# A hybrid decoder block on one core: the input projection of the first two x tiles in two halves of the model width

## The chip, the cores and the metric

The kernel runs on one core of one Trainium2 chip. A core has five engines with queues of their own: TensorE (PE in the rows; its weight loads are PEld), VectorE (DVE), ScalarE (ACT), GpSimd (POOL) and SyncE (SP), which here issues the large DMAs. They meet through semaphores. The metric is the device time of one execution in microseconds; less is better.

## What is computed

One layer over x of 1024 rows by 1024 columns, all in f32. The reference, cut to what matters here:

```python
mod = (silu(c) @ w_ada + b_ada)                      # 1024 -> 6 * 1024
sh1, sc1, g1, sh2, sc2, g2 = split(mod, 6)
h = rms_norm(x, norm1_g) * (1 + sc1) + sh1
q, k, v, u = split(h @ w_in)                         # 512, 128, 128, 512 columns
q, k = rope(rms_norm(q)), rope(rms_norm(k))          # angles = positions * inv_freq
a = sliding_window_attention(q, k, v, sinks)         # window 128
p = (window_mean(u, 2/4/8/16) - u) @ pool_w * pool_scale
x = x + g1 * (concat(a, p) @ w_o)
h2 = rms_norm(x, norm2_g) * (1 + sc2) + sh2
x = x + g2 * (square(relu(h2 @ w_mlp_in)) @ w_mlp_out)
```

## The kernel before

TensorE's products keep f32 accuracy by three products each: every operand is split into a high part (a cast to fp32r) and a low part (the operand less its high part), and high*high, high*low and low*high are added in PSUM. The casts are mostly ScalarE's (hi_... functions), the low parts VectorE's (lo_...).

**Order.** Nothing schedules this program: each engine's instructions stand in the order in which its block writes them, and semaphores (wait_ge) join the engines. An engine that waits holds all that stands behind it.

**Tiles.** x is worked in eight tiles of 128 rows. For each: square and root mean (square_x on ScalarE, root_x on GpSimd), scale (scale_x), transposes on TensorE (turn_x), h from the transposed tile with a1 and b1, one scalar per row of the transposed tile (make_h on VectorE for columns 0 to 511, make_h_half on ScalarE for the others), high and low parts of h, and the projection to u, q and k/v over KD = 8 blocks of 128 of the model width. u runs through window sums (pool_windows, with band matrices that GpSimd makes at the start) and a pool product (pool_out); q and k through norm, rope and transposes (turn_qk) to scores.

**The front.** Before h exists, b1 = sh1 and a1 = (1 + sc1) * norm1_g are needed. Both are 1024 to 1024 products of silu(c) with slices of w_ada. VectorE adds them up from eight pieces each (add_piece, [128, 1024], acc for sh1 and acc_sc for sc1), and TensorE sums the 128 partitions with one-column products (column_sum, L2075). The list stream sets the order of the loads into 12 buffers: eight pieces of sh1, eight of sc1, then w_in's u columns (wu, 4 pieces of two blocks) and its q, k and v columns (wqkv, 8 pieces of one block); x tiles 0 and 1 are asked for after the eighth. So nothing is projected before both vectors are complete. TensorE then runs project_u_first (L2238), project_qkv_first (L2274) and the second tile's project_u and project; products nobody reads (keep_clock, L2070) fill some of its waits. The later adaLN vectors are summed by VectorE in add_job_pieces between its other work for the tiles, by three lists of piece numbers (first_pieces, between_pieces, late_pieces), and loaded by JOB_LOADS.

**Two late steps.** angles (L1210) makes the rope angles on VectorE when tile 0 has been projected; sines (L876) follows on ScalarE. The band matrices differ for tile 0 (the window is cut at the start of the sequence), so GpSimd first makes that form (band_of, L1855) and rewrites it after tile 0's windows.

## Time and profile before

| | us |
|---|---|
| median of 3 runs | 938.44 (938.17 to 939.15) |
| the profiled execution | 939.17 |
| its span | 937.4 |
| TensorE busy | 915.0 |
| VectorE busy | 650.2 |
| ScalarE busy | 495.1 |
| GpSimd busy | 361.7 |

The span is the time from the first to the last instruction of one profiled execution, whose own time is 939.17; all rows have their times from the span's start. Busy times of engines overlap. A row of the timeline gives start, duration, engine, line, operation, output and inputs, and in brackets how long the engine had been idle and what ended that. The granted clock is TensorE's: 1.00 is 2.4 GHz and 0.50 is 1.2 GHz. A duration of a merged row runs from the first start to the last end of its x instructions; an f32 product of 128 columns is two of them.

### The profile page before, as it was taken

What the parts mean: (1) busy time and instruction counts of PE and PEld (TensorE: products, weight loads), DVE (VectorE), ACT (ScalarE), POOL (GpSimd) and SP (SyncE); (2) the same over time, 40 slices, a digit from 0 to 9 for tenths busy, and PEclk for the clock granted to TensorE, in tenths of its full rate; (3) what the DMA queues carried; (4) which work ended last, traced back from release to release, by engine and by line L of the source; (5) the groups of instructions that cost most, each with busy time, mean ns of one, the idle gap of its engine ahead of it and who ended that gap; (6) DMA issues with size and microseconds to landing.
All of it is one profiled execution on the core that took longest, in us unless ns stands there. A gap on an engine that the chain in (4) does not pass through costs nothing.

```text
span 937.4 us, 12606 instructions
## 1 busy us (share of the span) xinstructions
PE 915.0 (98%) x4387; PEld 765.5 (82%) x4387; DVE 650.2 (69%) x1001; ACT 495.1 (53%) x869; POOL 361.7 (39%) x347
## 2 busy tenths in 40 slices
PE   2999999999999999999999999999999999999998
PEld 2888888887888888888888888888888888888886
DVE  6978987888645778556555654445786666799896
ACT  2657888887655546554455544536334444333331
POOL 8162322243323446988888888721000000000000
PEclk9899999999999999999999999999999999999999
DMA  9943232235122423746555553349999538996772
GB/s 357 371 170 95 91 114 90 91 106 188 45 90 90 134 69 123 243 162 197 188 176 169 176 184 131 115 172 332 349 339 320 196 102 289 317 302 209 258 248 94
DMA packets 92271, 175.54 MB, mean 187 GB/s; under 512 B 9320, under 2 KB 26288, under 8 KB 92208
## 3 DMA queue, kind: packets, MB, share of 16 engines
q1 hardware_dynamic: 92096, 174.70, 55.0%
q8 instruction: 35, 0.57, 0.2%
q14 instruction: 28, 0.23, 0.1%
q10 hardware_dynamic: 112, 0.04, 0.0%
HBM read 136.95 MB, written 37.75 MB: 186 GB/s over the span
## 4 chain that ended last, share of the span: by engine, by line
PE 92%; DVE 4%; DMA 2%; SPq 1%; issue 1%; ACT 1%; POOL 0%; DVEq 0%
PE psum L2060 27%; PE psum L2062 27%; PE psum L2061 27%; PE psum L2056 3%; DMA raw<-in_w_ada 2%; PE psum L2154 1%; PE psum L2155 1%; PE psum L2158 1%; PE psum L2140 1%; DVE w_o_lo L1372 1%; PE psum L2230 1%; PE psum L2200 1%; PE psum L2173 1%; PE psum L2236 1%; DVE probs L1337 1%
## 5 line engine op out<-in xcount | busy, mean ns | idle before, releaser
L1115 ACT CAST down_operands<-down_raw 128x1024 fp32r<-128x1024 f32 x96 | 100.9, 1054 | 151.9 <-PE psum L2062 54.6
L2060 PE MATMUL psum<-down_operands 128*128 128x512 f32 x448 | 174.3, 389 | 0.0
L2061 PE MATMUL psum<-down_operands 128*128 128x512 f32 x448 | 174.3, 389 | 0.0
L2062 PE MATMUL psum<-down_operands 128*128 128x512 f32 x448 | 174.3, 389 | 0.0
L1775 DVE TENSOR_TENSOR down_operands<-down_raw,down_operands 128x1024 fp32r<-128x1024 f32 x93 | 112.5, 1220 | 19.5 <-ACT down_operands L1115 18.9
L2060 PE MATMUL psum<-h2T,w_operands 128*128 128x512 f32 x272 | 106.0, 390 | 0.1
L2062 PE MATMUL psum<-h2T,w_operands 128*128 128x512 f32 x272 | 105.9, 389 | 0.0
L2061 PE MATMUL psum<-h2T,w_operands 128*128 128x512 f32 x272 | 105.8, 389 | 0.0
L2060 PEld LDWEIGHTS psum<-down_operands 128*128 128x128 f32 x448 | 84.1, 188 | 17.6
L2062 PEld LDWEIGHTS psum<-down_operands 128*128 128x128 f32 x448 | 84.1, 188 | 17.4
L2061 PEld LDWEIGHTS psum<-down_operands 128*128 128x128 f32 x448 | 84.1, 188 | 17.3
L2012 POOL TENSOR_TENSOR w_operands<-raw,w_operands 128x512 fp32r<-128x512 f32 x56 | 84.2, 1505 | 35.6 <-ACT w_operands L1063 35.6
L2062 PE MATMUL psum<-t_sums_hi,w_operands 128*128 128x512 f32 x168 | 65.4, 389 | 0.0
L2060 PE MATMUL psum<-t_sums_hi,w_operands 128*128 128x512 f32 x168 | 65.4, 389 | 0.0
L2061 PE MATMUL psum<-t_sums_lo,w_operands 128*128 128x512 f32 x168 | 65.4, 389 | 0.0
L2060 PEld LDWEIGHTS psum<-h2T,w_operands 128*128 128x128 f32 x272 | 51.1, 188 | 11.1 <-issue 0.5
L2061 PEld LDWEIGHTS psum<-h2T,w_operands 128*128 128x128 f32 x272 | 51.1, 188 | 10.6
L2012 POOL TENSOR_TENSOR w_operands<-w_sums,w_operands 128x512 fp32r<-128x512 f32 x42 | 55.3, 1329 | 11.3 <-ACT w_operands L1063 11.3
L2062 PEld LDWEIGHTS psum<-h2T,w_operands 128*128 128x128 f32 x272 | 51.1, 188 | 10.5
L1063 ACT CAST w_operands<-w_sums 128x512 fp32r<-128x512 f32 x42 | 26.1, 623 | 55.9 <-PE psum L2062 52.5
L2060 PE MATMUL psum<-w_o_hi,mixT_hi 128*128 128x512 f32 x128 | 51.2, 400 | 0.0
L2062 PE MATMUL psum<-w_o_hi,mixT_lo 128*128 128x512 f32 x128 | 50.0, 391 | 0.0
(285 smaller groups left out, 1960.9 us busy)
## 6 DMA issues: line engine op xcount, KB each, us to landing
down_raw<-in_w_mlp_out SPq DMA_DIRECT2D x160, 256.0 KB, 4.3
down_raw<-act_scratch SPq DMA_DIRECT2D x112, 256.0 KB, 3.3
raw<-in_w_ada SPq DMA_DIRECT2D x32, 512.0 KB, 4.6
raw<-in_w_mlp_in SPq DMA_DIRECT2D x32, 512.0 KB, 5.0
act_scratch<-act_quads_a SPq DMA_DIRECT2D x64, 256.0 KB, 2.3
act_scratch<-act_quads_b SPq DMA_DIRECT2D x48, 256.0 KB, 3.6
slots<-in_w_ada SPq DMA_DIRECT2D x8, 512.0 KB, 10.6
xh<-in_x SPq DMA_DIRECT2D x8, 512.0 KB, 5.7
```

Source lines behind the costliest of these rows:

```text
L1063: nc.scalar.copy(w1op[:, w1_slot(b, name), 0, :, :], w1_quad(b, quad)).then_inc(w1_hi, 1)
L1115: nc.scalar.copy(o[:, 0, :, :], r[:, 0:2, :]).then_inc(op2_hi, 1)
L1337: ins = v.tensor_tensor_reduce(out=pr[:, kv, h, 0:w], in0=banks(4)[:, 256 * h:256 * h + w], in1=mask[:, m0:m0 + w], scale=1.0, scalar=-3e3 ...
L1372: v.tensor_tensor(wol[:, k, :], piece_at(place[("wo", k)]), woh[:, k, :].bitcast(F32), ALU.subtract).then_inc(wo_lo_dve, 1)
L1775: v.tensor_tensor(o[:, 1, :, :], r[:, 0:2, :], f32(o[:, 0, :, :]), ALU.subtract).then_inc(op2_lo_dve, 1)
L2012: g.tensor_tensor(o[:, 1, :, :], quad, o[:, 0, :, :].bitcast(F32), ALU.subtract).then_inc(w1_lo, 1)
L2056: return nc.tensor.transpose(o, i, ident[0:rows_, 0:rows_])
L2060: mm(o, wh, ah, start=first, stop=False, skip_group_check=adds)
L2061: mm(o, wh, al, start=False, stop=False, skip_group_check=adds)
L2062: return mm(o, wl, ah, start=False, stop=last, skip_group_check=adds)
L2140: ins = mm(o, qT[:, kv * G + h, :], k_, start=a == 0, stop=a == 1)
L2154: mm(bank(0), h[:, k, :], wih[:, k, QKV:IN], start=k == 0, stop=False)
```

## The change

The front is cut in two halves of the model width. Each double piece now has 512 columns of sh1 and the same 512 of sc1 (stream's mod pieces). After eight of them a1 and b1 are complete for blocks 0 to 3, and TensorE projects x tiles 0 and 1 over those blocks (project_u_half, project_qkv_half), leaving the sums open in PSUM: tile 1 gets banks of its own (u_bank, q_bank, kv_bank). The other eight pieces are summed meanwhile, and a second pass over blocks 4 to 7 ends the sums (project_qkv_second, then the u halves). The loads are interleaved to match. ScalarE makes the first half of h for both tiles, VectorE the second half of tile 0 in two steps. angles goes on VectorE behind the first sums (with one product in place of eight), sines into the front on ScalarE. GpSimd takes three of the casts (wu 1, wqkv 1 and 3), and makes the general band and a 16-column form for tile 0's first columns, used by extra narrow products. Two casts stand around the second x tile's square. keep_clock stands at other places with other counts. The adaLN sums of sh2, sc2 and g1 get a buffer each, and their pieces, loads and reductions move to later tiles.

```diff
-        stream = [("sh1", k) for k in range(KD)]
-        stream += [("sc1", k) for k in range(KD)]
-        stream += [("wu", k) for k in range(KD // 2)]
-        stream += [("wqkv", k) for k in range(KD)]
+        stream = [("mod", k) for k in range(KD)]
+        stream += [("wu", 0), ("wu", 1)]
+        stream += [("wqkv", k) for k in range(NK)]
+        stream += [("mod", KD + k) for k in range(KD)]
+        stream += [("wqkv", k) for k in range(NK, KD)]
+        stream += [("wu", 2), ("wu", 3)]
...
-        JOB_LOADS = (4, 4, 4, 3, 4, 4, 1, 0)
+        JOB_LOADS = (4, 2, 3, 4, 4, 5, 2, 0)
+        job_sums = (slots[:, NT - 1, :], slots[:, NT - 2, :], acc[:, :])
+        POOL_CASTS = ((1,), (1, 3))
...
                 load(n)
-                if n == 7:
+                if n == 2:
                     load_x(0)
+                if n == place[("wu", 1)]:
                     load_x(1)
...
+            square_x(0)
+            scale_x(0)
+            hi_wu(0)
+            make_h_half(0, 0)
+            hi_h(0, 0)
+            hi_wqkv(0)
+            square_x(1)
+            hi_wqkv(2)
+            scale_x(1)
+            make_h_half(1, 0)
             hi_h(1, 0)
+            sines()
...
+            sum_front(0)
+            angles()
+            shift_1(0)
             scale_1(0)
-            make_h(0, 0)
+            lo_wu(0)
+            lo_wu(1)
+            lo_h(0, 0)
+            for k in range(NK):
+                lo_wqkv(k)
+            sum_front(1)
+            lo_wqkv(4)
+            shift_1(1)
             scale_1(1)
+            make_h_front()
...
-            first_pieces = ([], [], (5,), (8,), (12, 13), (16,), (18, 19), (22,))
-            between_pieces = ([], [], [], (9,), (14,), (17,), (20,), (23,))
-            late_pieces = ((0, 1, 2, 3), (4,), (6, 7), (10, 11), (15,), [], (21,), [])
+            first_pieces = ([], [], (2,), (5,), (9,), (13, 14), (18,), (22,))
+            between_pieces = ([], [], [], (6,), (10,), (15,), (19,), (23,))
+            late_pieces = ([], (0, 1), (3, 4), (7, 8), (11, 12), (16, 17), (20, 21), [])
...
-                if t in (3, 5):
+                if t in (4, 6):
...
+            for n, fill in ((3, 8), (4, 6)):
+                pe.wait_ge(mod_summed, n)
+                keep_clock(fill, 3)
+            turn_x(0)
+            for n, fill in ((5, 4), (6, 5), (7, 2)):
+                pe.wait_ge(mod_summed, n)
+                keep_clock(fill, 3)
             pe.wait_ge(mod_summed, KD)
...
+            ins.then_inc(sc1_turned, 1)
+            keep_clock(8, 3)
...
+            project_u_half(0, 0)
+            project_qkv_half(0, 0, (q_part(0), kv_part(0)))
+            project_u_half(1, 0)
+            project_qkv_half(1, 0, (q_part(1), kv_part(1)))
+            keep_clock(4, 2)
+            for n, fill in ((15, 4), (16, 2)):
                 pe.wait_ge(mod_summed, n)
                 keep_clock(fill, 2)
...
+            pe.wait_ge(b1_second, 1)
+            pe.wait_ge(a1_ready, 2)
+            turn_x(1, NK, KD)
+            project_qkv_second()
+            project_u_half(0, 1)
+            project_u_half(1, 1)
+            pe.wait_ge(u_kept, 1)
+            turn_x(2)
+            project_qkv_half(1, 1, (q_part(1),))
             pool_windows(0)
-            turn_x(2)
-            pe.wait_ge(q_gained, 1)
-            project(bank(6), 0, AW, 1).then_inc(q_done, 1)
+            project_qkv_half(1, 1, (kv_part(1),))
             pool_out(0)
```

How instructions stand, at three places. First TensorE ahead of its first projection product, before (xh is the x tile, ones the vector of the column sums, the products of ident alone are keep_clock's):

```order
L2076 MATMUL psum<-ones,acc 128x1 [waits mod_summed]
L2076 MATMUL psum<-ones,acc 128x1 x7
L2056 MATMUL psum<-ident,xh 128x128 [waits x_scaled]
L2056 MATMUL psum<-ident,xh 128x128 x7
L2056 MATMUL psum<-ident,xh 128x128 [waits x_scaled,cols_ready]
L2056 MATMUL psum<-ident,xh 128x128 x7
```

and now:

```order
L2147 MATMUL psum<-ident 128x128 x5
L2130 MATMUL psum<-ident,xh 128x128 [waits x_scaled]
L2130 MATMUL psum<-ident,xh 128x128 x7
L2147 MATMUL psum<-ident 128x128 [waits mod_summed]
L2147 MATMUL psum<-ident 128x128 x3
L2147 MATMUL psum<-ident 128x128 [waits mod_summed]
L2147 MATMUL psum<-ident 128x128 x4
L2147 MATMUL psum<-ident 128x128 [waits mod_summed]
L2147 MATMUL psum<-ident 128x128
L2150 MATMUL psum<-ones,acc 128x1 [waits mod_summed]
```

The transposes of x tile 0 and 25 fill products have moved ahead of the first column sums, and those of tile 1 are gone from here. Second, VectorE behind its first eight pieces, before:

```order
L1255 COPY cols<-psum 128x72 [waits rows_turned]
L1205 TENSOR_SCALAR squares<-slots,small 128x1024 [waits raw_in8,mod_summed]
L1207 SCALAR_TENSOR_TENSOR squares<-slots,small,squares 128x1024 [waits raw_in9,mod_summed]
L1207 SCALAR_TENSOR_TENSOR squares<-slots,small,squares 128x1024 [waits raw_in10,mod_summed]
L1207 SCALAR_TENSOR_TENSOR squares<-slots,small,squares 128x1024 [waits raw_in11,mod_summed]
```

and now, from the last step of the angles:

```order
L1282 TENSOR_SCALAR probs<-probs 128x64 [waits own_dve]
L1313 TENSOR_TENSOR small<-psum,cols 128x4 [waits mod_turned,cols_ready]
L1323 TENSOR_TENSOR small<-psum,cols 128x4 [waits sc1_turned]
L1326 SCALAR_TENSOR_TENSOR small<-small,cols 128x4 [waits own_dve]
L1357 TENSOR_TENSOR w_in_lo<-slots,w_in_hi 128x2x512 [waits wu_hi,raw_in8]
L1357 TENSOR_TENSOR w_in_lo<-slots,w_in_hi 128x2x512 [waits wu_hi_pool,raw_in9]
L1350 TENSOR_TENSOR hT_lo<-xh,hT_hi 128x512 [waits h_hi]
L1363 TENSOR_TENSOR w_in_lo<-slots,w_in_hi 128x768 [waits wqkv_hi,raw_in10]
L1363 TENSOR_TENSOR w_in_lo<-slots,w_in_hi 128x768 [waits wqkv_hi_pool,raw_in11]
L1363 TENSOR_TENSOR w_in_lo<-raw,w_in_hi 128x768 [waits wqkv_hi,raw_in0]
L1363 TENSOR_TENSOR w_in_lo<-raw,w_in_hi 128x768 [waits wqkv_hi_pool,raw_in1]
L1255 TENSOR_SCALAR squares<-raw,small 128x1024 [waits raw_in2]
```

The second eight pieces now stand behind a wait for TensorE's column sums and seven low parts. Third, GpSimd around the roots of x tiles 0 and 1, before (one root for both, after three bands):

```order
L1858 AFFINE_SELECT band<-band 128x16 [waits own_pool]
L1861 AFFINE_SELECT band<-band 128x16 [waits own_pool]
L1870 TENSOR_SCALAR small<-small 128x2 [waits x_squared,own_pool]
L1872 TENSOR_TENSOR small<-small 128x2 [waits own_pool]
L1883 MEMSET band 128x1 x15
```

and now, from the end of the second band's successor:

```order
L1932 TENSOR_TENSOR band<-band,ident 128x128 [waits own_pool]
L1952 CAST w_in_hi<-slots 128x2x512 [waits raw_in9]
L1936 TENSOR_SCALAR small<-small 128x1 [waits x_squared]
L1938 TENSOR_TENSOR small<-small 128x1 [waits own_pool]
L1956 CAST w_in_hi<-slots 128x768 [waits raw_in11]
L1956 CAST w_in_hi<-raw 128x768 [waits raw_in1]
```

The root of tile 0 stands after two bands of five operations each; the second root is a wait of its own with two casts behind it.

## Rows read from the trace of the kernel before

**Rows 1.** The page: the span, and TensorE's clock in 40 slices.

```profile
span 937.4 us, 12606 instructions
PEclk9899999999999999999999999999999999999999
```

**Rows 2.** TensorE's waits, 0 to 110: line, releaser, us in total, times, longest.

```profile
PE psum L2076 <- DVE acc L1207: 3.5, 1, 3.5
...
PE psum L2056 <- DVE kT L1367: 0.5, 1, 0.5
```

**Rows 3.** The timeline, TensorE up to its first projection product.

```profile
20.57 3.68 PE L2056 MATMUL psum<-ident,xh 128*128 128x128 f32 x16 [0.81 <-ACT xh L725]
...
24.04 2.08 PE L2073 MATMUL psum<-ident 128*128 128x128 f32 x14
...
28.39 1.83 PE L2076 MATMUL psum<-ones,squares 128*128 128x1 f32 x15
...
31.95 2.07 PE L2230 MATMUL psum<-w_in_hi,hT_hi 128*128 128x512 f32 x4 [0.61 <-ACT hT_hi L744]
```

**Rows 4.** Windows: length, busy times, granted clock, DMA share, GB/s.

```profile
31.00:32.00 1.00, 0.39 (x5) 0.20 (x3) 0.96 (x4) 0.90 (x3) 0.00 (x0) 0.64 1.07 398
32.00:33.00 1.00, 1.00 (x3) 0.81 (x4) 1.00 (x2) 1.00 (x4) 0.00 (x0) 0.50 1.03 399
...
38.00:39.00 1.00, 1.00 (x5) 0.77 (x4) 1.00 (x2) 1.00 (x3) 0.00 (x0) 0.95 1.03 402
```

**Rows 5.** The timeline, VectorE: sums, low parts of u, of h, of qkv, angles.

```profile
12.22 3.93 DVE L1207 SCALAR_TENSOR_TENSOR acc<-slots,small,acc 128x1024 f32<-128x1024 f32 x3
...
33.17 1.22 DVE L1294 TENSOR_TENSOR w_in_lo<-slots,w_in_hi 128x1024 fp32r<-128x1024 f32 x1
34.31 0.69 DVE L1287 TENSOR_TENSOR hT_lo<-xh,hT_hi 128x512 fp32r<-128x512 f32 x1
...
37.29 3.56 DVE L1300 TENSOR_TENSOR w_in_lo<-slots,w_in_hi 128x768 fp32r<-128x768 f32 x4
...
52.17 0.74 DVE L1225 SCALAR_TENSOR_TENSOR probs<-probs 128x64 f32<-128x64 f32 x3
```

**Rows 6.** The timeline, ScalarE: first square, a cast of h, a half tile.

```profile
15.37 1.06 ACT L720 ACTIVATE pooledT<-xh 128x1024 bf16<-128x1024 f32 x1 [12.76 <-DMA xh<-in_x]
...
31.28 0.62 ACT L744 CAST hT_hi<-xh 128x512 fp32r<-128x512 f32 x1
31.80 1.50 ACT L734 ACTIVATE xh<-psum,small 128x128 f32<-128x128 f32 x4
```

**Rows 7.** The timeline, GpSimd: one operation in a gap of VectorE, one beside its sums.

```profile
7.85 0.29 POOL L1861 TENSOR_SCALAR_AFFINE_SELECT band<-band 128x128 f32<-128x128 f32 x1
...
12.43 1.23 POOL L1858 TENSOR_SCALAR_AFFINE_SELECT band<-band 128x128 f32<-128x128 f32 x1
```

**Rows 8.** The timeline, TensorE: tile 1's first u products, tile 2's first.

```profile
48.85 0.40 PE L2154 MATMUL psum<-w_in_hi,hT_second 128*128 128x512 f32 x1
...
49.09 0.39 PE L2155 MATMUL psum<-w_in_lo,hT_second 128*128 128x512 f32 x1
...
65.98 0.47 PE L2154 MATMUL psum<-w_in_hi,hT_hi 128*128 128x512 f32 x1
```

**Rows 9.** DMA queues from 8 to 9: packets, MB, share; q10 is ScalarE's.

```profile
q10 hardware_dynamic: 6, 0.00, 0.6%
```

**Rows 10.** The instructions on acc: GpSimd's cast of 1024 columns.

```profile
L1913 POOL CAST g_hi<-acc x1: 1042/1042/1042, 193.0 to 193.0; 128x1024 fp32r<-128x1024 f32 x1
```

**Rows 11.** Windows: tile 4, after 120.

```profile
120.00:143.00 23.00, 23.00 (x148) 20.48 (x147) 20.20 (x55) 19.67 (x49) 6.42 (x9) 1.00 0.34 114
```

More of the change, by code:

```diff
@@ L323, in build @@
         out_quad = [sem("out_quad0"), sem("out_quad1"), sem("out_quad2")]
-        own = {e: sem(f"own_{e}") for e in ("act", "dve", "pool")}
+        own = {e: sem(f"own_{e}") for e in ("dve", "pool")}
         block = ctx.enter_context(nc.Block())
@@ new lines, in sum_front @@
+            def sum_front(half):
+                sums = acc_sc if half else acc
+                for k in range(KD):
+                    if k >= 1:
+                        dve.wait_ge(mod_summed, front_summed(KD * half + k - 1))
+                    if k < KD - 1:
+                        add_piece(sums[:, :], ("mod", KD * half + k), k, mod_summed)
+                    else:
+                        a = landed(dve, ("mod", KD * half + k))
+                        for m in range(2):
+                            cut = slice(512 * m, 512 * m + 512)
+                            v.scalar_tensor_tensor(out=sums[:, cut], in0=a[:, cut], scalar=silu[:, k:k + 1],
+                                                   in1=sums[:, cut], op0=ALU.mult, op1=ALU.add).then_inc(mod_summed, 1)
+                    if half == 0 and k == 1:
+                        dve.wait_ge(rows_in, 16 * 4)
+                        v.tensor_copy(rows[64:72, :], posi[64:72, :]).then_inc(posf_ready, 1)
+                    if half == 0 and k == 2:
+                        dve.wait_ge(rows_turned, 1)
+                        v.tensor_copy(cols[:, :], psum[:, 0, 0:72]).then_inc(cols_ready, 1)
+                    if half == 1 and k == 1:
+                        lo_h(1, 0)
@@ L1875, in _, with hi_wqkv @@
+            def hi_wqkv(k):
+                a = landed(pool, ("wqkv", k))
+                g.tensor_copy(wih[:, k, 0:QKV], a[:, 0:QKV]).then_inc(wqkv_hi[1], 1)
+            inv = np.float32(ROPE_THETA) ** (-np.arange(0, ROT_DIM, 2, dtype=np.float32) / np.float32(ROT_DIM))
+            for f in range(HALF):
+                ins = g.memset(inv_row[:, f:f + 1], float(inv[f]))
+            ins.then_inc(ident_made, 1)
             for i, w in enumerate(POOL_WINDOWS):
-                own_p.step(g.memset(band[:, i, 0:P], 1.0 / w))
+                own_p.step(g.memset(band[:, i, :], 1.0 / w))
@@ L1877, in _ @@
+            for s in range(MAX_WINDOW):
+                own_p.step(g.memset(band_first[:, s:s + 1], float(np.float32(1.0) / np.float32(s + 1))))
             own_p.wait()
-            for i, w in enumerate(POOL_WINDOWS):
-                if i == NP - 1:
-                    pool.wait_ge(x_squared, 2)
-                    root(rx[:, 0:2], ssx[:, 0:2], D, x_root)
-                for s in range(w - 1):
-                    own_p.step(g.memset(band[:, i, s:s + 1], float(np.float32(1.0) / np.float32(s + 1))))
-                own_p.wait()
-                band_of(i, band[:, i, 0:P], 0)
-                own_p.step(less_token(i, P))
-                own_p.wait()
-                own_p.step(g.memset(band[:, i, P:BAND], 1.0 / w))
-                own_p.wait()
-                band_of(i, band[:, i, P:BAND], P)
+            own_p.step(g.affine_select(out=band_first, in_=band_first, compare_op=ALU.is_ge, fill=0.0, base=0,
+                                       pattern=[[1, MAX_WINDOW]], channel_multiplier=-1))
@@ L2216, in _, with hi_hi, lo_hi @@
-            turn_x(1)
-            keep_clock(3, 2)
-            for n, fill in ((13, 4), (14, 4), (15, 2)):
+            pe.wait_ge(mod_summed, KD + 1)
+            for k in range(NK):
+                ins = column_sum(bank(2)[:, k:k + 1], acc, NK + k)
+            ins.then_inc(sc1_turned, 1)
+            keep_clock(8, 3)
+            def hi_hi(o, t, k, a, b):
+                return mm(o, hT(t)[0][:, k, :], wih[:, k, a:b], start=k == 0, stop=False)
+            def lo_hi(o, t, k, a, b):
+                return mm(o, hT(t)[1][:, k, :], wih[:, k, a:b], start=False, stop=False)
@@ new lines, in project_qkv_half @@
+            def project_qkv_half(t, half, parts):
+                pe.wait_ge(h_hi, h_step(t, half))
+                for k in range(NK * half, NK * half + NK):
+                    if (t, k) == (0, 3):
+                        turn_x(1, 0, NK)
+                    hi_made(pe, wqkv_hi, k)
+                    for o, a, b, _ in parts:
+                        hi_hi(o, t, k, a, b)
+                    pe.wait_ge(h_lo, h_step(t, half))
+                    for o, a, b, _ in parts:
+                        lo_hi(o, t, k, a, b)
+                    pe.wait_ge(wqkv_lo, k + 1)
+                    for o, a, b, done in parts:
+                        ins = hi_lo(o, t, k, a, b)
+                        if k == KD - 1:
+                            ins.then_inc(done, 1)
```

435 lines of the change are left out of this document (221 added, 214 removed).

## The prediction

> **What bounds the kernel now.** I read the page first: the span is 937.4 us and its PEclk row is 9 in nearly every slice [rows 1], so TensorE works almost without a break and anything that makes its dense work start earlier shifts the whole kernel. Then TensorE's waits before 110 us [rows 2]: behind the wait for the first transpose, which costs nothing by itself, stand the first column sums (3.5 us on VectorE's sums), and after that only waits under a microsecond. Then the timeline: until 31.95 TensorE does only column sums, transposes and products that nobody reads; the first projection product stands at 31.95 and from there no gap is seen [rows 3]. Last the windows of the clock [rows 4]: the mean is 0.64 at 31 to 32, 0.50 at 32 to 33 and 0.95 at 38 to 39, so the first projection runs some 6.2 us at half clock (1.2 GHz instead of 2.4), which costs 3.1 us. The yardstick for the change is the stretch from 31.95 to 65.98, where the third x tile's u projection starts [rows 8]: 34.0 us. What follows it is the same work in both kernels.
>
> **The start of the first half.** The transfers of 512 KB land 1.29 us apart (the first before the sum at 5.07, x tile 0 as the ninth just before its square at 15.37 [rows 6]). Now x tile 0 is the fourth and lands at 8.9; the eighth double piece lands at 15.3. VectorE's sums run at 1.31 us each (3.93 for 3 [rows 5]) and end at 17.3. The row vectors land on ScalarE's queue between 8 and 9 us [rows 9], so their cast, now after piece 1, ends at 8.9 and delays nothing by more than the copy.
>
> TensorE then has 14 clock-keeping products from the third sum on (10.4), the 8 transposes, 11 more products and 8 column sums before anything can be scaled. A pass takes 0.23 us at half clock and about 0.12 at full (3.68 for 16 transposes against 2.08 for 14 passes, two passes to a product [rows 3]). The clock rose about 3.9 us after the transposes began at 20.57 (PEclk reads 1.00 there, but the passes fall from 0.23 to 0.15), and 6.2 us after 31.95; from 10.4 that gives 14.3 to 16.6, and I take 15.7. The 14 products then end at 16.5, transposes 17.5, 11 products at 0.245 at 20.2, column sums (8 at 0.24) at 22.1. The root of x must be there by 16.5. GpSimd has ten band operations ahead of it. An operation that meets a sum takes 1.23 us instead of 0.29 [rows 7]; seven of ten so give a root at about 13.6 and the scaled tile at 14.7: not last. Bounds: all ten slow give 16.0 and 17.1, 0.6 us late. From 22.1: two small VectorE steps 0.5, ScalarE's half tile 1.50 and cast 0.62 [rows 6]: first product at **24.8**, 7.2 us earlier than before. The angles (about ten steps of 0.2 to 0.25 us, 0.74 for three [rows 5]) lie between 17.3 and 19.7, under TensorE's fill; if that cover were gone they would cost 2.4.
>
> **The first half itself.** Per tile 12 products each of u and q at 0.2275 (48.85 to 49.09 and on [rows 8]) and 12 of k and v at 0.12: 6.9 us, for two tiles 13.8. VectorE after 22.6: low parts of u twice 1.2, of h 0.7, of the qkv pieces 0.9 each [rows 5]. The second and fourth qkv casts stand on GpSimd behind the root of x tile 1, and that behind ScalarE's square, which now comes after cast 0: root at 27.5, cast of 768 columns 0.8 (1024 take 1.04 [rows 10]). VectorE waits 1.9 us for it; the bounds are 0 and 2.7. TensorE meets little of that (0.1), but x tile 1 is transposed only before the fourth piece (30.8), so ScalarE has its half cast at 33.5, and TensorE waits 1.2. First half ends at **40.4**, all at full clock.
>
> **Between the halves.** VectorE starts the second sums at 31.2: 0.8, low part of h 0.7 with 0.3 wait, six at 1.31 and a split one of 1.4: 42.2. Data is not last: the pieces land up to 34. TensorE has 10 more products (2.45) after 40.4 and stands at 42.9, 0.7 us behind the sums it could already have taken. Column sums 44.8, two small steps with their hand-overs 45.5, first two blocks of h 46.2, cast 0.4: second half starts at **46.7**. The gap is 6.2 us. Before, there was none. Here is where the early start goes.
>
> **The second half** is 13.8 us, x tile 2's transposes 0.9, windows 1.1 (now 1.4, four more narrow products), pool product 1.0 and the transposes of q and k 0.7, with 0.5 of waits for the high parts of h and of qkv piece 7: third u projection at **65.1**. ScalarE's queue (square of x 2 ahead of the squares of q) and the load of x 2, which now waits for the low part of the second half (47.8) and is 2.5 to 5 us under way, would stall it only if x 2 came after 55; I take nothing, bound 0 to 1.5.
>
> The sum against 31.95 to 65.98: start -7.2, half clock gone -3.1, gap +6.2, waits in the first half +1.3, transposes of x tile 1 now inside +1.0, windows +0.3, waits in the second half +0.5, rounding +0.1: **-0.9 us**. Off the path and free: the freed fix-up of the bands on GpSimd, the table load for the sines (covered by ScalarE's wait for h), the reordered loads. The profiled execution took 939.17 with its span of 937.4, against a median of 938.44; I take the difference off the median: 937.5 (a profiled execution would show 938.3, its span 936.5).
>
> **Later tiles.** Four adaLN sums leave VectorE's third-tile stretch and come back in tile 5 (five where two stood), and the reductions move from tiles 3 and 5 to 4 and 6. VectorE is busy 20.20 of 23 us at 120 to 143, TensorE 23.00 [rows 11]. One reduction (1.3) leaves 1.5 there. The waits that could vanish are 0.5 (kT) [rows 2]. I take 0, bounds -0.5 and +1.5.
>
> **A rule against it.** In the trace the clock rose while TensorE did only transposes (20.57 on [rows 3]). The Trainium skill, TensorE: Matmul & The Clock Gate, Part 4, says that transpose mode does not count as busy the same way; this trace disagrees. By the rule the stretch between the halves would hold only one-column sums and four idle transposes, which is the second rival.
>
> **The rivals.**
> 1. *The clock falls at the first half (slower).* Before, it fell at 31.3, after eight column sums (28.39 [rows 3]), four fill products and 0.6 us of waiting; now the same with eight fill products and 1.1 us of waiting. If it falls, 6.2 us at half clock cost 3.1, first half ends at 43.4 and everything follows: +2.1, **940.6**. It decides by whether eight fill products are enough. For it: the same pattern. Against: 11 products ahead of the sums and twice the fill.
> 2. *It falls between the halves.* 42.9 to 46.7 holds sums, waits and four transposes. Cost, since part hides under the waits for high parts, 2.2: **939.7**. Against: dense products stand on both sides.
> 3. *More overlap (faster).* The clock rises at 14.3 and the GpSimd cast is not waited for: first product 24.0, VectorE's sums end at 39.5, and TensorE's own work is last; with the first x tile's wait of 1.2 gone too, the second half starts at 44.8: -2.8, **935.6**.
> 4. *VectorE in tiles 4 to 6* becomes late: +1.5 on the sum, **939.0**.
> That the split changes nothing because weights land late is excluded by the landings above.
>
> **How the numbers follow.** Likeliest 0.42: 937.5, with 936.2 to 939.2 as its own range. Rival 1 0.20, rival 2 0.10, rival 3 0.22, rival 4 0.06. A measurement of this kernel can tell about 0.2% (1.9 us) from no change, so the line is at 936.6 and 940.3. Faster: 0.12 of the first case and 0.21 of rival 3, 0.33. Slower: 0.18 of rival 1, 0.05 of rival 2, 0.02 each of the first and rival 4, 0.27. Same 0.40. The range leaves out about a tenth on each side: 934.8 to 941.2.
>
> **What would show it.** First projection product near 24.8 (below 24: rival 3; above 26: GpSimd's root was late). Granted clock 1.00 from there to the end (rival 1: 0.50 for six windows). A gap of projection products between about 40.4 and 46.7, ended by column sums; if VectorE's sums end before 41, the fill products are the cost. Third u projection at 65.1. Most wrong I would be if the gap is under 3 us, or if both halves run at half clock.

## The result, and the profile of the changed kernel

| us | before | changed |
|---|---|---|
| median of 14 runs each | 937.51 (936.66 to 939.15) | 939.53 (937.73 to 940.45, and one of 3304.46) |
| the same two kernels, measured again | 937.33 (30 runs) | 939.31 (10 runs) |
| ratio | | 1.002, 95% interval 1.0012 to 1.0027; measured again 1.001 to 1.003 |
| third u projection at full clock (variants with wide column sums) | 63.72 | 64.98 |

The changed kernel is 2.0 us slower; 0.9 us faster was forecast. One run of the first comparison took 3304.46 us and was the profiled one; so the profile after is that of the same kernel measured again: 940.12 us, span 938.4, mean granted clock 0.998. The last line of the table is explained with the experiments.

The span and the clock in 40 slices, from the page of the changed kernel. They answer to [rows 1]; the 8 in the second slice is gone, yet the span is longer.

```profile
span 938.4 us, 12712 instructions
PEclk9999999999999999999999999999999999999999
```

TensorE up to the third u projection, from the timeline of the changed kernel (start, duration, engine, line, operation, output and inputs, count, and in brackets the idle time before and what ended it). These rows answer to [rows 3, 8].

```profile
11.27 6.21 PE L2147 MATMUL psum<-ident 128*128 128x128 f32 x28 [0.87 <-DVE acc L1257]
17.31 1.04 PE L2130 MATMUL psum<-ident,xh 128*128 128x128 f32 x8
18.18 2.62 PE L2147 MATMUL psum<-ident 128*128 128x128 f32 x22
20.64 1.84 PE L2150 MATMUL psum<-ones,acc 128*128 128x1 f32 x16
22.34 2.03 PE L2147 MATMUL psum<-ident 128*128 128x128 f32 x16
25.12 1.19 PE L2311 MATMUL psum<-w_in_hi,hT_hi 128*128 128x512 f32 x4 [0.75 <-ACT hT_hi L785]
...
34.61 1.20 PE L2311 MATMUL psum<-w_in_hi,hT_second 128*128 128x512 f32 x4 [1.29 <-ACT hT_second L785]
...
41.72 2.39 PE L2147 MATMUL psum<-ident 128*128 128x128 f32 x20
43.95 1.84 PE L2150 MATMUL psum<-ones,squares 128*128 128x1 f32 x16
46.36 0.63 PE L2130 MATMUL psum<-ident,xh 128*128 128x128 f32 x4 [0.57 <-DVE small L1316]
47.57 2.66 PE L2311 MATMUL psum<-w_in_hi,hT_hi 128*128 128x512 f32 x8 [0.59 <-ACT hT_hi L792]
...
67.23 0.47 PE L2231 MATMUL psum<-w_in_hi,hT_hi 128*128 128x512 f32 x1
```

The first projection product stands at 25.12 (31.95 before), so the front does start early. The first half runs to 41.72. Then come ten products nobody reads (x20 passes), the second column sums at 43.95, four transposes and, at 47.57, the second half. A stretch of 5.85 us holds no projection product and the kernel before had no such stretch. The third u projection stands at 67.23 against 65.98 [rows 8].

The clock at the start of the second half, from the windows of the changed kernel (window, length, busy time of PE, PEld, DVE, ACT, POOL with counts, granted clock, DMA share, GB/s), answering to [rows 4]:

```profile
46.00:47.00 1.00, 0.63 (x4) 0.42 (x4) 0.87 (x5) 0.00 (x0) 0.00 (x0) 1.00 0.00 0
47.00:48.00 1.00, 0.43 (x2) 0.38 (x3) 1.00 (x4) 0.65 (x2) 0.00 (x0) 0.95 0.00 0
48.00:49.00 1.00, 1.00 (x5) 0.90 (x4) 1.00 (x2) 1.00 (x3) 0.00 (x0) 0.50 0.00 0
...
51.00:52.00 1.00, 1.00 (x6) 0.81 (x6) 1.00 (x2) 1.00 (x4) 0.00 (x0) 0.84 0.88 336
```

The half clock (1.2 GHz) has not gone; in this execution it stands in the second half, 47.9 to 51.3, and not in the first projection. Before the fall TensorE did column sums, waited, did four transposes and waited again.

VectorE around its second eight pieces, from the timeline of the changed kernel:

```profile
28.65 1.48 DVE L1363 TENSOR_TENSOR w_in_lo<-slots,w_in_hi 128x768 fp32r<-128x768 f32 x1 [1.78 <-POOL w_in_hi L1956]
...
41.80 1.42 DVE L1296 SCALAR_TENSOR_TENSOR squares<-slots,small,squares 128x512 f32<-128x512 f32 x2
...
45.83 0.16 DVE L1316 TENSOR_TENSOR small<-psum,cols 128x4 f32<-128x4 f32 x1 [1.75 <-PE psum L2150]
```

The sums end at about 43.1, and TensorE takes them at 43.95, behind its fill.

### The profile page after: what moved, and what is told of

Read it like the earlier page. It is cut to its first block, busy times and chain, and to the rows that moved or that the text cites. A ratio compares the mean times of both kernels' runs of the same rounds, so it can differ in the third digit from the quotient of the medians.

```text
span 3302.7 us, 12712 instructions
## 1 busy us (share of the span) xinstructions
PE 3288.9 (100%) x4447; PEld 1833.7 (56%) x4447; DVE 657.0 (20%) x988; ACT 500.5 (15%) x875; POOL 341.2 (10%) x331
## 4 chain that ended last, share of the span: by engine, by line
PE 100%; DMA 0%; DVE 0%; ACTq 0%; issue 0%; ACT 0%
PE psum L2135 28%; PE psum L2134 27%; PE psum L2136 27%; PE psum L2130 4%; PE psum L2215 2%; PE psum L2231 1%; PE psum L2235 1%; PE psum L2232 1%; PE psum L2147 1%; PE psum L2314 1%; PE psum L2311 1%; PE psum L2317 1%; PE psum L2284 1%; PE psum L2251 1%; PE psum L2188 0%; PE psum L2190 0%
## 5 line engine op out<-in xcount | busy, mean ns | idle before, releaser
L2134 PE MATMUL psum<-down_operands 128*128 128x512 f32 x448 | 492.7, 1100 | 0.0
L2135 PE MATMUL psum<-down_operands 128*128 128x512 f32 x448 | 492.4, 1099 | 0.0
L2136 PE MATMUL psum<-down_operands 128*128 128x512 f32 x448 | 486.3, 1085 | 0.0
L2135 PE MATMUL psum<-h2T,w_operands 128*128 128x512 f32 x272 | 298.9, 1099 | 0.0
L2136 PE MATMUL psum<-h2T,w_operands 128*128 128x512 f32 x272 | 298.2, 1096 | 0.0
L2134 PE MATMUL psum<-h2T,w_operands 128*128 128x512 f32 x272 | 296.2, 1089 | 0.0
L2135 PEld LDWEIGHTS psum<-down_operands 128*128 128x128 f32 x448 | 196.8, 439 | 173.7 <-issue 173.7
L2134 PEld LDWEIGHTS psum<-down_operands 128*128 128x128 f32 x448 | 190.0, 424 | 180.7 <-issue 180.7
L2136 PEld LDWEIGHTS psum<-down_operands 128*128 128x128 f32 x448 | 189.0, 422 | 173.1 <-issue 173.1
L2135 PE MATMUL psum<-t_sums_lo,w_operands 128*128 128x512 f32 x168 | 184.5, 1098 | 0.0
L2136 PE MATMUL psum<-t_sums_hi,w_operands 128*128 128x512 f32 x168 | 184.4, 1098 | 0.0
L2134 PE MATMUL psum<-t_sums_hi,w_operands 128*128 128x512 f32 x168 | 182.9, 1088 | 0.0
L2136 PEld LDWEIGHTS psum<-h2T,w_operands 128*128 128x128 f32 x272 | 118.1, 434 | 105.4 <-issue 105.4
L2135 PEld LDWEIGHTS psum<-h2T,w_operands 128*128 128x128 f32 x272 | 116.2, 427 | 108.5 <-issue 108.5
L2134 PEld LDWEIGHTS psum<-h2T,w_operands 128*128 128x128 f32 x272 | 114.8, 422 | 106.0 <-issue 105.9
L2134 PE MATMUL psum<-w_o_hi,mixT_hi 128*128 128x512 f32 x128 | 143.5, 1121 | 0.0
L2136 PE MATMUL psum<-w_o_hi,mixT_lo 128*128 128x512 f32 x128 | 140.2, 1095 | 0.0
L2135 PE MATMUL psum<-w_o_lo,mixT_hi 128*128 128x512 f32 x128 | 140.2, 1095 | 0.0
L2136 PEld LDWEIGHTS psum<-t_sums_hi,w_operands 128*128 128x128 f32 x168 | 73.4, 437 | 65.4 <-issue 65.4
```

Source lines behind the costliest of these rows:

```text
L2134: mm(o, wh, ah, start=first, stop=False, skip_group_check=adds)
L2135: mm(o, wh, al, start=False, stop=False, skip_group_check=adds)
L2136: return mm(o, wl, ah, start=False, stop=last, skip_group_check=adds)
```

## The experiments

Three causes could be behind the missing 2.9 us. The fill products, in the front and in the gap, may hold TensorE up. The clock may have been mis-sized on both sides: worth less in the kernel before than the 3.1 us credited, and lost again between the halves. Or the later tiles may have become slower (theory B in the expectations).

Ten runs of one kernel lie up to 3.5 us apart, mostly by the clock, so a difference between two medians is uncertain by about 1 us; the smaller ones below are carried by the rows and not by the medians.

The later tiles could be dropped from the two traces alone: from the third u projection to the end of the span the changed kernel takes 938.4 - 67.23 = 871.2 us, the kernel before 937.4 - 65.98 = 871.4.

**The changed kernel again** (no edit).

> The changed kernel once more, to read its rows. Theory A (the clock): TensorE runs a few us of the first half at half clock, so the granted clock of the whole execution is 0.998 or 0.996 and the span 937 to 939; the first projection product stands near 24.8 and the third u projection between 65.1 (never at half clock) and 67.2. Theory B (later tiles): the front ends near 65.1 at full clock and the loss of 1 to 2 us is in TensorE waits between 70 and 230.

Measured: 939.31 against 937.33. All rows above are from this run.

**The kernel before again** (no edit, one execution), since its first profile was one execution out of many.

> The kernel before once more, to read its clock in another execution. If its usual half-clock stretch at the first projection is 6.8 us, as in the profiled execution of 939.2 us, the granted clock is 0.996 and the time near 939; if it is usually 3.4 us, 0.998 and near 937.4. The second would mean that 1.7 us of the clock gain I counted was mostly not there to be had.

Its timeline, TensorE's first projection and the third u projection; then the windows around the clock's fall:

```profile
31.91 2.08 PE L2230 MATMUL psum<-w_in_hi,hT_hi 128*128 128x512 f32 x4 [0.20 <-ACT hT_hi L744]
...
64.13 0.47 PE L2154 MATMUL psum<-w_in_hi,hT_hi 128*128 128x512 f32 x1
```

```profile
33.00:34.00 1.00, 1.00 (x4) 0.81 (x3) 1.00 (x2) 0.97 (x3) 0.00 (x0) 0.50 1.04 402
34.00:35.00 1.00, 1.00 (x5) 0.80 (x5) 0.98 (x3) 1.00 (x2) 0.00 (x0) 0.93 1.02 396
```

Measured: 937.27, span 935.5. The first product is where it was, but the half clock lies at 30.7 to 34.1 and not at 31.3 to 38.1, and the third u projection stands 1.85 us earlier than in [rows 8]. The trace that the prediction was made from held the longer of two stretches. Of the 93 runs of the kernel before that were made beside the experiments, 10 have a mean granted clock of 0.996 as that trace (median 939.12), 45 have 0.998 as this one (937.71), and 38 have 0.999 or 1.000 (936.73). The yardstick was one execution in nine.

**Without the fill in the gap:**

```diff
-            keep_clock(4, 2)
-            for n, fill in ((15, 4), (16, 2)):
-                pe.wait_ge(mod_summed, n)
-                keep_clock(fill, 2)
```

> The changed kernel without the ten fill products between the two halves. Theory A1: TensorE reaches VectorE's finished second sums 0.7 us late because of them, so the gap shrinks by about 0.7 us where the first half ran at full clock and by up to 2.4 us where it ran at half; 0.7 to 2.4 us faster. Rival: without them the clock falls between the halves and costs 1.7 to 3.1 us; 0 to 2 us slower. If VectorE's sums are last by more than 2.4 us: no difference in time.

TensorE's timeline of that kernel:

```profile
24.04 1.20 PE L2311 MATMUL psum<-w_in_hi,hT_hi 128*128 128x512 f32 x4 [1.51 <-ACT hT_hi L785]
...
41.55 1.95 PE L2150 MATMUL psum<-ones,squares 128*128 128x1 f32 x16 [0.74 <-DVE squares L1296]
...
45.28 2.84 PE L2311 MATMUL psum<-w_in_hi,hT_hi 128*128 128x512 f32 x8 [0.50 <-ACT hT_hi L792]
```

Measured: 938.16 (ratio to before 1.0008, 0.9998 to 1.0017), 1.15 less than the changed kernel. From the first product to the second column sums it takes 41.55 - 24.04 = 17.5 us, with the fill 43.95 - 25.12 = 18.8: the fill holds the sums up by 1.3. (In the trace with the fill TensorE starts them 0.8 us after VectorE's last step at 43.1; without it four of the eight start already when the first half of the last piece is summed.) It does not keep the clock either: this execution fell at 44.5, the one with fill at 47.9. So the fill in the gap is a cause, with about half of the loss.

**Without the fill in the front:**

```diff
             turn_x(0)
-            for n, fill in ((5, 4), (6, 5), (7, 2)):
-                pe.wait_ge(mod_summed, n)
-                keep_clock(fill, 3)
```

> The changed kernel without the eleven fill products between the transposes of x tile 0 and the first column sums. If they stand on the path (the transposes are later than VectorE's first sums), the first projection product comes 2 to 2.7 us earlier and the time falls by 1 to 2.5 us. If the sums are last, nothing moves there. Rival: the clock falls or rises later without them and a half-clock stretch of 3.4 to 6.8 us costs 1.7 to 3.4 us; up to 2 us slower.

VectorE's last step of the angles and the first step on the column sums, then TensorE, from that kernel's timeline:

```profile
21.15 0.20 DVE L1282 TENSOR_SCALAR probs<-probs 128x64 f32<-128x64 f32 x1
21.25 0.15 DVE L1313 TENSOR_TENSOR small<-psum,cols 128x4 f32<-128x4 f32 x1
```

```profile
17.42 1.95 PE L2150 MATMUL psum<-ones,acc 128*128 128x1 f32 x16 [1.14 <-DVE acc L1296]
...
23.92 1.78 PE L2308 MATMUL psum<-w_in_hi,hT_hi 128*128 128x512 f32 x4 [2.66 <-ACT hT_hi L785]
```

Measured: 940.04 (1.0022, 1.0012 to 1.0032); no gain. The column sums stand 3.2 us earlier than in the changed kernel's trace, but the angles now end last on VectorE, at 21.3, and TensorE waits 2.66 us. After that wait the clock was at half (24.3 to 27.7), as well as at the start of the second half (48.2 to 51.6). Fill and angles are two covers of one stretch: without the fill alone the first product stays (23.92, against 24.04 in the trace before).

**More fill ahead of the first half:**

```diff
-            keep_clock(8, 3)
+            keep_clock(12, 3)
```

> The changed kernel with twelve fill products instead of eight behind the first column sums, which closes the 1.1 us of waiting for the first half of h. Theory A: the half-clock stretch at the first half is gone or shorter more often, granted clock 1.000 in more executions, 1 to 2 us faster than the changed kernel. Rival: the one-column sums decide, not the waiting: no difference within 0.5 us.

Measured: 938.96 (1.0013, 1.0004 to 1.0022), not told apart from the changed kernel. The clock was already full in the first half, and it fell between the halves as before (47.2 to 50.6). Three of its ten runs have a mean clock of 1.000.

**Wide column sums in the changed kernel.** The vector of ones becomes 128 (64 in the second sums) equal columns; its readers take the first of each. The result is the same, the number of instructions too.

```diff
-                return mm(o, sums[:, k * P:(k + 1) * P], ones[:, 0:1].bitcast(F32), start=True, stop=True)
+                return mm(o, sums[:, k * P:(k + 1) * P], ones[:, 0:o.shape[1]].bitcast(F32), start=True, stop=True)
```

> The changed kernel with column sums of 128 equal columns in the first group and 64 in the second instead of 1 (same number of passes; VectorE reads one column of each). Theory C: the clock falls at the start of the second half because the one-column sums ahead of it leave the array idle; with wide ones the half-clock stretch (3.4 us, costing 1.7) is gone in most executions, granted clock 1.000, 1 to 1.7 us faster than the changed kernel. Rival: the 1.2 us of true waiting decides; clock 0.998 as before, same time.

```profile
24.09 1.20 PE L2311 MATMUL psum<-w_in_hi,hT_hi 128*128 128x512 f32 x4 [0.85 <-ACT hT_hi L785]
...
42.92 1.90 PE L2150 MATMUL psum<-ones,squares 128*128 128x64 f32 x16
...
46.59 1.99 PE L2311 MATMUL psum<-w_in_hi,hT_hi 128*128 128x512 f32 x8 [0.58 <-ACT hT_hi L792]
...
64.98 0.47 PE L2231 MATMUL psum<-w_in_hi,hT_hi 128*128 128x512 f32 x1
```

```profile
48.00:49.00 1.00, 1.00 (x5) 0.87 (x6) 1.00 (x3) 1.00 (x2) 0.00 (x0) 1.00 0.07 16
```

Measured: 937.96 (1.0011, 1.0001 to 1.002), 1.35 less than the changed kernel. Sixteen passes take 1.90 to 1.95 us instead of 1.84, so the width is nearly free. The granted clock stays at 1.00; the first eight products of the second half take 1.99 instead of 2.66. From the start of the second half to the third u projection it is 64.98 - 46.59 = 18.4 us against 67.23 - 47.57 = 19.7: the stretch at half clock costs 1.3. Eight of its ten runs have a mean clock of 1.000; of the changed kernel's 23 ordinary runs three have. Those three took 937.73 to 937.85, which is this kernel's time at that clock. So the changed kernel without any fall takes 937.8, still 1.1 more than the kernel before without any (936.73).

**Wide column sums in the kernel before** (the same edit at its two places), which takes the half clock out of the yardstick.

> The kernel before with column sums of 128 equal columns in place of 1. Theory C: its half-clock stretch at the first projection (3.4 to 6.8 us) follows the one-column sums at 28.4; with wide ones it is gone, granted clock 1.000, the third u projection at about 62.5 instead of 64.1, 1.5 to 1.8 us faster than before (near 935.6). Rival: the waits for VectorE's pieces at 26 to 28 decide: same as before.

TensorE in the first projection (the first product, one with a wait ahead of it, the first product of q and k/v, which ends the u projection), and VectorE's low parts, which feed it:

```profile
32.07 1.21 PE L2230 MATMUL psum<-w_in_hi,hT_hi 128*128 128x512 f32 x4 [0.72 <-ACT hT_hi L744]
...
34.57 0.73 PE L2236 MATMUL psum<-w_in_lo,hT_hi 128*128 128x512 f32 x2
...
38.12 0.50 PE L2230 MATMUL psum<-w_in_hi,hT_hi 128*128 128x512 f32 x2
...
63.72 0.47 PE L2154 MATMUL psum<-w_in_hi,hT_hi 128*128 128x512 f32 x1
```

```profile
35.14 2.36 DVE L1294 TENSOR_TENSOR w_in_lo<-slots,w_in_hi 128x1024 fp32r<-128x1024 f32 x2
37.42 3.56 DVE L1300 TENSOR_TENSOR w_in_lo<-slots,w_in_hi 128x768 fp32r<-128x768 f32 x4
```

The end of the same u projection in the kernel before, first in the trace that the prediction was made from, then in the execution profiled again:

```profile
40.38 0.50 PE L2230 MATMUL psum<-w_in_hi,hT_hi 128*128 128x512 f32 x2
```

```profile
38.53 0.51 PE L2230 MATMUL psum<-w_in_hi,hT_hi 128*128 128x512 f32 x2
```

Measured: 936.86 (0.9991, 0.9982 to 1.0001); all ten runs at 1.000. The third u projection stands at 63.72. Against that, the execution with the short stretch (64.13) lost 0.4 us and the one of [rows 8] (65.98) lost 2.3, not 3.1. By the medians of the 93 runs the short stretch costs 1.0 (937.71 against 936.73) and the long one 2.4, so 0.4 is the low end.

The u projection shows why. Its 24 products take 38.12 - 32.07 = 6.05 us at full clock, 40.38 - 31.95 = 8.43 with the long stretch and 38.53 - 31.91 = 6.62 with the short one: the half clock costs 2.4 and 0.6 there, and nothing is won or lost behind it (from its end to the third u projection all three take 25.60). Two things make up the difference from 3.1 and 1.7 us, half of each stretch. At full clock TensorE is held up: 24 products 0.23 us apart would take 5.5, and it waits some 0.5 us more in small pieces, the longest for VectorE's low parts (ahead of 34.57), which VectorE makes without a pause from 31.6 on, in the same places as in the run at half clock (from 31.4). At half clock it merely works where it would otherwise wait. And of the short stretch (30.7 to 34.1) only 2.2 us lie on the projection, the rest on fill products and a wait. So both sides of the clock were mis-sized, the credit and the loss.

**Both cures in the changed kernel** (wide sums, no fill in the gap).

> Wide column sums and no fill products between the halves. Theory C with A1: both gains, 2 to 3 us faster than the changed kernel (936.5 to 937.5). Rival: without the fill the clock falls in spite of the wide sums; 938.2 as without the fill alone.

Measured: 937.0 (0.9999, 0.999 to 1.0008), the third u projection at 63.62. The two costs add: 1.35 and 1.0. This is level with the kernel before.

**GpSimd's cast ahead of the second root**, on top of the last one:

```diff
             hi_wu_second()
-            root_x(1)
             hi_wqkv(1)
+            root_x(1)
             hi_wqkv(3)
```

> As the last, and GpSimd's cast of wqkv 1 ahead of the root of x tile 1. VectorE's wait of 1.8 us for that cast goes. If VectorE's chain sets the start of the second half, that start comes 0.8 to 1.8 us earlier and the time falls by as much; if the transposes of x tile 1 and ScalarE's half of h are last, nothing moves, or the later root costs up to 0.3 us.

VectorE's timeline of that kernel:

```profile
29.57 0.96 DVE L1363 TENSOR_TENSOR w_in_lo<-raw,w_in_hi 128x768 fp32r<-128x768 f32 x1 [0.79 <-POOL w_in_hi L1956]
...
33.87 0.69 DVE L1350 TENSOR_TENSOR hT_second<-xh,hT_second 128x512 fp32r<-128x512 f32 x1 [1.32 <-ACT hT_second L785]
```

Measured: 936.49 (0.9993, 0.9984 to 1.0003), 0.5 less than the last one, which ten runs each do not tell apart. The wait of 1.78 us for GpSimd is cut to 0.79, and a wait for ScalarE's high part of h of tile 1 has grown from 0.56 to 1.32: the early start is nearly used up one row further on. The profiled execution had a stretch of 6.8 us at half clock (44.1 to 51.0) in spite of the wide sums, and took 939.07, so these make falls rarer and do not exclude them. TensorE waits 0.75 us for the sums here, which it did not with the fill; the kernel with both cures has the same wait and kept its clock in the profiled execution, so the wait alone does not decide either.

**That low part one piece later**, on top of the last one. This follows from the row above: VectorE asks for h of tile 1 behind its second piece, before ScalarE has it.

```diff
-                    if half == 1 and k == 1:
+                    if half == 1 and k == 2:
                         lo_h(1, 0)
```

> Wide column sums, no fill between the halves, cast first, and VectorE's low part of tile 1's first half of h one piece later, so that its wait of 1.3 us for ScalarE's cast is filled by a piece. If VectorE's sums set the start of the second half, it comes 0.7 (until TensorE itself is last) to 1.3 us earlier: 935.2 to 935.8 where the clock holds. Rival: TensorE waits for the low part instead and gains nothing.

VectorE and TensorE of that kernel:

```profile
31.60 1.28 DVE L1257 SCALAR_TENSOR_TENSOR squares<-slots,small,squares 128x1024 f32<-128x1024 f32 x1
32.89 0.86 DVE L1350 TENSOR_TENSOR hT_second<-xh,hT_second 128x512 fp32r<-128x512 f32 x1
```

```profile
40.03 1.89 PE L2150 MATMUL psum<-ones,squares 128*128 128x64 f32 x16
...
43.71 2.00 PE L2311 MATMUL psum<-w_in_hi,hT_hi 128*128 128x512 f32 x8 [0.58 <-ACT hT_hi L792]
...
62.20 0.47 PE L2231 MATMUL psum<-w_in_hi,hT_hi 128*128 128x512 f32 x1
```

Measured: **935.17** (0.9979, 0.9968 to 0.9989), the best of all, 2.1 under the kernel before and 4.1 under the changed one. Against the kernel before with wide sums too (936.86) it is 1.7: that is what the split is worth once its gap is mended. The wait is gone, the column sums follow the first half with no wait at all, and the gap is down to 43.71 - 40.03 = 3.7 us: sums, hand-overs, four transposes and a cast.

**The kernel with the cast first (936.49) without the front fill.**

> Wide column sums, cast first, none of the fill products between the transposes of x tile 0 and the first sums nor between the halves. The first projection product comes 2 to 2.6 us earlier (near 22) and the time falls by 1.5 to 2.6 us if the clock holds; rival: the clock falls at the first half, as it did without this fill and with one-column sums (at 24 to 27.4), and 1.7 us of it is given back.

Measured: 937.93 (1.0007, 0.9997 to 1.0016). The sums stand at 17.46 and the first product still at 23.95 behind a wait of 2.65, since the angles are last again; none of its ten runs had the clock full throughout, against six of ten with the fill; the profiled one was at half clock from 43.1 to 50.0, between the halves. The fill in the front earns its place, by 1.4 us; why a fill that stands more than 20 us earlier should matter to the clock there, no run shows.

**The angles back in their old place**, in the changed kernel:

```diff
             sum_front(0)
-            angles()
             shift_1(0)
...
+            angles()
             norm_k(0)
```

(and sines behind scale_x(2) on ScalarE).

> The changed kernel with the angles and sines at their old place, one part undone. In the changed kernel the angles (3.5 us on VectorE, 17.87 to 21.34) end 0.35 us before the first column sums: covered by the eleven fill products on TensorE. So nothing moves at the front (first product within 0.4 us); VectorE has the steps in a stretch at 55 to 60 where it waits: same time within 0.5 us. Rival: there they delay the norm of k and with it the q and k transposes: 1 to 2 us slower.

```profile
23.36 1.20 PE L2311 MATMUL psum<-w_in_hi,hT_hi 128*128 128x512 f32 x4 [0.75 <-ACT hT_hi L785]
...
58.68 1.10 PE L2130 MATMUL psum<-ident,xh 128*128 128x128 f32 x8 [1.83 <-ACT u_rows L880]
```

Measured: 940.26 (six runs; 1.0038, 1.0025 to 1.0051), 1.0 worse than the changed kernel. At the front the first product comes earlier (23.36), but the early angles are worth more than that: TensorE's transposes of x tile 2 now wait for ScalarE's copy of u. **With everything else on top** (the best kernel, no front fill, angles back):

> Wide column sums, cast first, low part later, no fill before the first sums nor between the halves, and angles back at their old place. If fill and angles cover each other (each alone changes nothing: without the fill TensorE waited 2.65 us for h behind the angles), both gone give a first product near 21.5 and the second half 1.5 to 2.4 us earlier than with the low part later alone: 933 to 934 if the clock holds. Rival: the second tile's x or the clock is last: 935 or more.

```profile
42.10 1.99 PE L2308 MATMUL psum<-w_in_hi,hT_hi 128*128 128x512 f32 x8 [0.58 <-ACT hT_hi L792]
...
54.65 1.09 PE L2130 MATMUL psum<-ident,xh 128*128 128x128 f32 x8 [2.33 <-ACT u_rows L880]
...
63.05 0.47 PE L2231 MATMUL psum<-w_in_hi,hT_hi 128*128 128x512 f32 x1
```

ScalarE in the same kernel:

```profile
53.43 0.69 ACT L911 ACTIVATE trig<-probs 128x64 f32<-128x64 f32 x4 [1.59 <-DVE probs L1282]
54.03 1.05 ACT L880 COPY u_rows<-psum 128x512 f32<-128x512 f32 x2
```

Measured: 936.25 (0.9993, 0.9983 to 1.0002). The sines wait for the angles and hold up the copies of u, which TensorE needs before it transposes x tile 2. The second half starts 1.6 us before that of the best kernel, and the wait of 2.33 at 54.65 takes it all back. I had expected 933 to 934. The first product stands at 22.35, so with both covers gone the front does start 1.6 us earlier than in the best kernel (23.92); the place behind the projection is what costs. Whether sines behind the copies of u would mend it, no run shows.

## Why the prediction was right in most of its steps and wrong in its sum

**The start, 24.8: right.** Measured 25.12 here, and 24.04 in the run without the gap fill, whose code is the same up to that point; here the clock rose later (the first 28 fill passes took 6.21 us, there 4.76), and TensorE's column sums were last. The root of x was not last.

**The first half, 24.8 to 40.4: 1.0 short.** Measured 25.12 to 41.72, 16.6 instead of 15.6. The waits come to 1.6 instead of 1.3 (1.29 for tile 1's half, 0.30 for a low part), and the rest are small breaks between products.

**The gap, 40.4 to 46.7: right in size, 5.85 instead of 6.3.** That VectorE's sums end at 42.2 (43.1) was right as well, and that TensorE's fill stands later than they do; the 0.7 between them is what the trace has (43.1 to 43.95, 0.8), but the fill costs 1.3, because half of the sums could have started before VectorE's last step.

**The second half, 18.4 us to the third u projection: right at full clock** (18.4 with wide sums), though its parts were not: the windows with their extra narrow products take 1.74 us from 62.51 to 64.25 (before 0.97, 54.31 to 55.28), so 0.8 more and not 0.3. A product of 2 columns takes as long there as one of 16 (0.14 us from its start to the next product's), so narrower ones save nothing. The waits that I had counted there at 0.5 were not seen.

**The clock between the halves: the rival of 0.10.** It is what the usual execution does: the profiled ones of the changed kernel, without the gap fill, without the front fill, with more fill and with the angles back all have a stretch at half clock there, and 20 of 23 runs of the changed kernel have a mean clock under 0.999. The rival had 939.7, and 939.31 to 939.53 is what came, but that the numbers meet is partly luck: its price of 2.2 was measured at 1.3, and it was set on a sum that still held the credit of 3.1. The argument against it, that dense products stand on both sides, was no argument: the falls began behind column sums and waits, and making only the sums wide took the clock to 1.000 in eight runs of ten. The Trainium skill, TensorE: Matmul & The Clock Gate, Part 4, says that transpose mode does not count as busy the same way. The four transposes in the gap stayed in the kernel with wide sums and the clock stayed up. In [rows 3] the clock did not rise during the transposes, as the prediction has it, but right behind them (3.68 us for their 16 passes, all at half clock, then 2.08 for 14 fill passes). In the execution profiled again the 16 took 3.55, and the last of them ran at full clock already. So these traces disagree with the page and speak for the width of the sums. They do not clear the rest: two later kernels with wide sums (the cast first, and no front fill) fell here too, after the same transposes and after a wait of 0.75 us for the sums, and without the front fill no run of ten kept the clock.

**The half clock gone, -3.1: the step that failed.** The prediction said of the first projection that it "runs some 6.2 us at half clock", "which costs 3.1 us", and took all of it back. With the stretch taken out of the kernel before, it gave 0.4 us in the profiled usual execution (1.0 by the medians) and 2.3 in the one of [rows 8]. Most of the error is that the stretch was the long one, which one execution in nine has; a third of the usual one lies ahead of the projection. The rest is that half of 6.2 holds only where TensorE waits for nothing at full clock, and there it waits some 0.5 us, mostly for VectorE's low parts ([rows 5] had them, 3.56 for four without a pause).

The prediction could have seen part of this in its own terms. Its pieces for the kernel before come to 13.8 + 13.8 + 0.9 + 1.1 + 1.0 + 0.7 = 31.3 us at full clock; with 3.1 that makes 34.4, and 34.0 was measured. In the sum this was hidden by the 1.0 for the transposes of x tile 1, four of which stand in the gap and were counted there too. The path of the changed kernel itself was forecast well for full clock: 65.1, and 64.98 was measured. What was wrong is what it was compared with, and the clock in its second half.

Put together at full clock, where nothing of the clock is in it, the sum of the prediction without its credit was -0.9 + 3.1 = +2.2, and 64.98 - 63.72 = +1.3 was measured. To that the clock adds its own balance: 1.3 lost in the changed kernel, 0.4 in the usual execution of the kernel before. It makes 1.26 + 1.27 - 0.41 = 2.1 against the 2.0 of the medians. (The 67.23 of the profiled execution holds 1.0 more, by which its first product was late.) The medians by clock give the same in other parts: 1.1 at full clock, 1.6 lost to the clock in the changed kernel, 0.6 in the kernel before. The change moved 8 us of start into 9 us of gap, waits and additional work.

One more choice moved the number: the difference was read against an execution of 939.17 and then taken off a median of three runs, 938.44, which the larger sample has at 937.51. That yardstick was 0.9 too high; the kernel came out 2.0 over the forecast of 937.5.

Of the other rivals, the fall at the first half did not come in the changed kernel's profiled execution; it came when the eleven products ahead of the sums were taken out, which that rival had named as the first thing against it. More overlap did not come by itself, but it can be had: the best kernel, at 935.17, lies close to the 935.6 given for it, by the way described there, with a shorter wait for GpSimd and none for ScalarE's high part. Its second half starts at 43.71, where that rival had 44.8; that the times meet is partly luck, since the rival's too held the credit of 3.1 and the high yardstick. VectorE in tiles 4 to 6 was not late: 871.2 against 871.4.

## What to carry to other kernels

A stretch at half clock costs only what TensorE could have done in it: before crediting half its length, see how much of it lies on products of the path and whether another engine feeds them, and take the stretch's length from several executions, since it varies from one to the next. A split that starts dense work earlier pays for it with a second hand-over, so count what stands in the gap, take the fill out of it and make its one-column products wide. And where two covers lie over one stretch (fill and angles here), removing one shows little; move the row that is waited for by one place and look at what is last next.

## What the runs showed of the hardware

- The stretches at half clock were of two lengths: about 3.4 us (30.7 to 34.1 in one execution of the kernel before, 47.9 to 51.3 in one of the changed) and about 6.8 (31.3 to 38.1 in the other of the kernel before, 44.1 to 51.0 with the cast first). The mean granted clock of an execution, 1.000, 0.998 or 0.996, told nearly all of the spread between executions: 937.8, 939.35 and 940.45 in the changed kernel.
- A one-column f32 product takes as long as one of 64 or 128 columns (0.115 to 0.12 us a pass). With the wide ones all ten runs of the kernel before kept the clock, against 38 of 93 runs without.
- One execution in 24 of the changed kernel took 3304 us, with TensorE slow all along: its products of 512 columns followed each other every 0.84 us and not every 0.23, while the granted clock was recorded as 1.000. No experiment was made on it, and its cause is open.
- The start of the first product differed by 1.1 us (24.04 and 25.12) between two executions of code that is the same up to there, because the first 28 fill passes took 4.76 us in one and 6.21 in the other; a difference of that size in one trace is not an effect of an edit.
